# Pooling means by trailing sums on VectorE and the layer norm's scale taken behind the mix, in a two-layer float32 trunk on one core

## The reference, cut to what matters

```python
def spatial_gating(u, v, ln_g, ln_b, w_s, b_s):          # branch A
    v = layer_norm(v, ln_g, ln_b)                        # over 512 channels
    w = where(mask[None], w_s, 0)                        # 4 groups of 128x128, masked by chunks of 64
    mixed = einsum('gts,bnsgc->bntgc', w, vb) + b_s      # mixes 128 positions
    return u * mixed

def multiscale_pool(xb, w_pool, scale):                  # branch B, one window per group of 128 channels
    for g, win in enumerate((2, 4, 8, 16)):
        count = minimum(t + 1, win)
        pooled.append((csg - lagged) / count - xf[:, :, g])   # mean of the last win positions, minus x
    y = einsum('bsgc,gcd->bsgd', pooled, w_pool)
    return y * scale
```

## Time and profile before

| what | value |
|---|---|
| median of 3 runs | 1374.77 us (1374.53 to 1376.07) |
| the profiled execution | 1375.41 us, of which its span is 1373.6 us |
| TensorE's granted clock, mean | 0.997 |
| TensorE busy | 1363.1 us |
| VectorE busy | 690.6 us |
| ScalarE, GpSimd busy | 561.3 and 553.9 us |

### The profile page before, as it was taken

One profiled execution on the slowest core, in us unless ns is written; L12 is line 12 of the kernel. 1 busy time (PEld: TensorE's weight loads), 2 busy tenths in 40 slices (PEclk: granted clock), 3 DMA queues, 4 the chain that ended last, 5 costly groups with the idle time before them and its releaser, 6 DMA issues.

```text
span 1373.6 us, 16132 instructions
## 1 busy us (share of the span) xinstructions
PE 1363.1 (99%) x6508; PEld 1150.1 (84%) x6508; DVE 690.6 (50%) x1051; ACT 561.3 (41%) x871; POOL 553.9 (40%) x233
## 2 busy tenths in 40 slices
PE   8999999999999999999999999999999999999998
PEld 7888888888888888888888888888888888888887
DVE  6977455255543333255767574451555532243743
ACT  5554454355552222224443654542555422222241
POOL 1334242443434444445354342424433344444443
PEclk9999999999999999999999999999999999999999
DMA  7313122232223333333343222222222233333232
GB/s 208 97 54 108 55 85 81 89 92 78 92 77 92 94 106 92 108 104 94 93 126 97 70 92 63 90 64 92 92 78 77 88 96 92 100 101 107 95 102 95
DMA packets 75354, 127.60 MB, mean 93 GB/s; under 512 B 8848, under 2 KB 45968, under 8 KB 75280
## 3 DMA queue, kind: packets, MB, share of 16 engines
q1 hardware_dynamic: 74048, 126.02, 29.8%
q10 hardware_dynamic: 1232, 0.55, 0.1%
HBM read 124.45 MB, written 2.10 MB: 92 GB/s over the span
## 4 chain that ended last, share of the span: by engine, by line
PE 95%; DVE 3%; ACT 1%; DMA 1%; SPq 0%; issue 0%; POOL 0%; DVEq 0%; ACTq 0%
PE ps L484 30%; PE ps L486 30%; PE ps L485 30%; DVE n_t L1456 1%; PE ps L753 1%; PE ps L687 1%; PE ps L789 1%; PE ps L674 1%; ACT w_hi L961 0%; DMA x<-x_in 0%; DVE h_lo L1315 0%; SPq L399 0%; DMA par<-par_in 0%; PE ps L565 0%; DVE xh L1482 0%
## 5 line engine op out<-in xcount | busy, mean ns | idle before, releaser
L459 POOL TENSOR_TENSOR w_lo<-w_raw,w_hi 128x1024 fp32r<-128x1024 f32 x222 | 547.3, 2469 | 776.4 <-ACT w_hi L961 776.2
L484 PE MATMUL ps<-h_hi,w_hi 128*128 128x512 f32 (+1 forms) x1096 | 427.3, 390 | 0.7 <-POOL w_lo L459 0.7
L486 PE MATMUL ps<-h_hi,w_lo 128*128 128x512 f32 (+1 forms) x1096 | 425.2, 388 | 0.0
L485 PE MATMUL ps<-h_lo,w_hi 128*128 128x512 f32 (+1 forms) x1096 | 425.0, 388 | 0.0
L961 ACT ACTIVATE w_hi<-w_raw 128x1024 fp32r<-128x1024 f32 x227 | 238.3, 1054 | 169.5 <-PE ps L486 167.7
L484 PEld LDWEIGHTS ps<-h_hi,w_hi 128*128 128x128 f32 x1096 | 205.9, 188 | 42.5 <-issue 0.9
L486 PEld LDWEIGHTS ps<-h_hi,w_lo 128*128 128x128 f32 x1096 | 205.8, 188 | 42.5
L485 PEld LDWEIGHTS ps<-h_lo,w_hi 128*128 128x128 f32 x1096 | 205.9, 188 | 40.8
L1757 DVE SCALAR_TENSOR_TENSOR m_part<-th,ps 128x512 f32<-128x512 f32 x48 | 33.0, 687 | 236.9 <-PE ps L486 236.8
L1179 ACT ACTIVATE th<-ps 128x512 f32<-128x512 f32 x48 | 28.7, 597 | 182.0 <-PE ps L486 182.0
L484 PE MATMUL ps<-w_hi,act_hi 128*128 128x512 f32 (+1 forms) x192 | 74.8, 390 | 4.5 <-DVE w_lo L1315 4.5
(11 more groups left out here) (334 smaller groups left out, 1969.2 us busy)
## 6 DMA issues: line engine op xcount, KB each, us to landing
w_raw<-w_in SPq DMA_DIRECT2D x172, 512.0 KB, 3.5
w_raw<-w_in SPq DMA_DIRECT2D x124, 128.0 KB, 2.4
w_raw<-w_in SPq DMA_DIRECT2D x36, 256.0 KB, 3.1
x<-x_in SPq DMA_DIRECT2D x8, 256.0 KB, 5.9
w_raw<-w_in SPq DMA_DIRECT2D x32, 64.0 KB, 2.1
out_x<-x SPq DMA_DIRECT2D x7, 256.0 KB, 4.1
rows<-rows_in SPq DMA_DIRECT2D x2, 768.0 KB, 5.7
p_raw<-p_in SPq DMA_DIRECT2D x2, 512.0 KB, 4.4
```

What stands on the lines that cost most here:

```text
L459: pool.tensor_tensor(w_lo_t[s][:], w_raw_t[s][:], w_hi_t[s][:].bitcast(F32), ALU.subtract).then_inc(w_lo_made, 1)
L484: pe.matmul(o, a_hi, b_hi, start=first, stop=False, skip_group_check=skip)
L485: pe.matmul(o, a_hi, b_lo, start=False, stop=False, skip_group_check=skip)
L486: return pe.matmul(o, a_lo, b_hi, start=False, stop=last, skip_group_check=skip)
```

## The change

- The bx products read h (after `h_made`), with weights as the stationary operand, so that the result stands by features in bank g, in the order bx3, bx2, bx1, bx0. ScalarE copies each to `xb`, which has 16 zero columns ahead of each group.
- VectorE sums windows by doubling: `trail(g)` makes g + 1 adds of the array with itself shifted by 1, 2, 4 and 8 columns, corrects the first 16 columns by a table, and multiplies by 1/window and subtracts x. `windows`, `window_tables` and their tables go. The edge table is four small operations in `constants_taken`.
- `pool_high` and `pool_split` make the parts from `xb`, groups 3, 2, 1, 0; the pool products run as groups 0 to 3, after bz1.
- `norm_scaled` goes. The mixing products run on the plain normalized values; two products with a matrix of ones sum the mixing weights into bank 5, `mix_off` is that sum by the shift plus the bias, and `mix_t` is the product by the scale plus `mix_off`. Scale and shift come as columns by a transpose in `rope_rows`, copied to `ln_col`.
- The load of these rows moves from before av3 to before av2 on SP. Queues of ScalarE and VectorE are written in a new order.

```diff
-    names = [f"lat{i}" for i in range(4)] + [f"av{i}" for i in range(4)] + [f"bx{i}" for i in range(4)]
+    names = [f"lat{i}" for i in range(4)] + [f"av{i}" for i in range(4)] + [f"bx{i}" for i in (3, 2, 1, 0)]
...
-ROWS_BY = "av3"
+ROWS_BY = "av2"
...
-        bx_hi, bx_lo = plan(0, 16, ("bx_hi", [TB, SEQ], F32R), ("bx_lo", [TB, SEQ], F32R))
+        xb, trail_a, trail_b = plan(0, 13, ("xb", [G, WIN], F32), ("trail_a", [WIN], F32), ("trail_b", [WIN], F32))
...
-        vn_hi, vn_lo, rows = plan(36, 58, ("vn_hi", [TB, SEQ], F32R), ("vn_lo", [TB, SEQ], F32R),
-                                  ("rows", [3, SEQ], F32))
+        vn_hi, vn_lo, rows, mix_off, ln_t = plan(
+            36, 58, ("vn_hi", [TB, SEQ], F32R), ("vn_lo", [TB, SEQ], F32R), ("rows", [SEQ], F32),
+            ("mix_off", [G, P], F32), ("ln_t", [P], F32))
...
+            whole = {"bx": lambda: S_BX[i], "bz": lambda: S_BZ[i], "cz": lambda: S_CZ[i], "gb": lambda: S_M1 + 3 * i,
...
-                        sync.dma_start(rows[:], rows_in[l].partition_broadcast(P)).then_inc(rows_loaded, 16)
+                        sync.dma_start(ln_t[0:2 * G, :], rows_in[l, 0:2].rearrange("u (g p) -> (u g) p", p=P)).then_inc(
+                            rows_loaded, 16)
+                        sync.dma_start(rows[:], rows_in[l, 2].partition_broadcast(P)).then_inc(rows_loaded, 16)
...
+                pe.wait_ge(rows_loaded, (l + 1) * 32)
+                pe.transpose(ps[:, 2 * 512 + P:2 * 512 + P + 2 * G], ln_t[0:2 * G, :], ident[0:2 * G, 0:2 * G])
...
-            def windows(l, g, b):
...
-                pe.wait_ge(pool_made, after(l * G + g))
+                pe.wait_ge(pool_made, after(l * G + 3 - g))
...
-                for i in range(4):
-                    project_rows(l, f"bx{i}", i, hx_hi, hx_lo, 0)
+                for i in (3, 2, 1, 0):
+                    w_hi, w_lo = chunk(l, f"bx{i}")
+                    for k in range(KD):
+                        if i == 3:
+                            pe.wait_ge(h_made, after(l * KD + k))
+                        last = mm3(bank(i), w_hi[:, k, :], w_lo[:, k, :], tile(h_hi, k), tile(h_lo, k), k == 0,
+                                   k == KD - 1)
+                    last.then_inc(done(l, f"bx{i}"), 1)
...
-                pe.wait_ge(h_made, after(l * KD + KD - 1))
                 project(l, "bz0", 7)
                 w_hi, w_lo = chunk(l, "vp")
                 pe.wait_ge(lat_made, after(l * 3))
                 for t in range(TB):
-                    pe.wait_ge(bx_made, after(l * TB + t))
+                    pe.wait_ge(bx_copied, after(l * G + 3 - t))
                     mm3(bank(t), tile(ckvn_hi, t, P), tile(ckvn_lo, t, P), w_hi[:, 0:G, :],
                         w_lo[:, 0:G, :]).then_inc(v_ready, 1)
-                if l == 0:
-                    pe.wait_ge(windows_made, after(0))
+                project(l, "bz1", 4)
                 for g in range(G):
-                    if g < 3:
-                        pe.wait_ge(lat_made, after(l * 3 + g))
-                    else:
-                        pe.wait_ge(v_made, after(l * TB))
-                    windows(l, g, WINDOW_BANKS[g])
-                pe.wait_ge(v_made, after(l * TB + 1))
-                project(l, "bz1", 1)
+                    pe.wait_ge(v_made, after(l * TB + g))
+                    pool_product(l, g, g)
+                pe.wait_ge(lat_made, after(l * 3 + 2))
+                project(l, "bz2", 6)
+                w_hi, w_lo = chunk(l, "mix")
+                pe.matmul(bank(5), ones_r[:], w_hi[:, 0:G, :], start=True, stop=False)
+                pe.matmul(bank(5), ones_r[:], w_lo[:, 0:G, :], start=False, stop=True).then_inc(wsum_ready, 1)
+                pe.wait_ge(ln_made, after(l * TB + TB - 1))
                 for g in range(G):
-                    if g < 2:
-                        pe.wait_ge(v_made, after(l * TB + g + 2))
-                    pool_product(l, g, 2 + g)
-                project(l, "bz2", 6)
-                w_hi, w_lo = chunk(l, "mix")
-                pe.wait_ge(ln_made, after(l * TB + TB - 1))
-                for g, b in enumerate(MIX_BANKS):
-                    if g:
-                        pe.wait_ge(pooled, after(l * G + g - 1))
+                    pe.wait_ge(pooled, after(l * G + g))
                     for t in range(TB):
-                        last = mm3(ps[:, b * 512 + t * P:b * 512 + (t + 1) * P], vn_hi[:, t, g * P:(g + 1) * P],
+                        last = mm3(ps[:, g * 512 + t * P:g * 512 + (t + 1) * P], vn_hi[:, t, g * P:(g + 1) * P],
                                    vn_lo[:, t, g * P:(g + 1) * P], w_hi[:, g, :], w_lo[:, g, :])
                     last.then_inc(mix_ready if g < G - 1 else done(l, "mix"), 1)
-                pe.wait_ge(pooled, after(l * G + 3))
+                pe.wait_ge(off_made, after(l))
                 project(l, "bz3", 5)
...
-                        if t != 1:
-                            pe.wait_ge(mix_taken, after(l * G + max(t - 1, 0)))
+                        pe.wait_ge(mix_taken, after(l * G + t))
...
-                weights_up_to(l, "bx0")
+                weights_up_to(l, "bx3")
...
                         act.wait_ge(*end_of(l, "av2"))
-                        weights_up_to(l, "bx1")
+                        weights_up_to(l, "bx2")
                 act.wait_ge(*end_of(l, "av3"))
-                weights_up_to(l, "bx2")
+                weights_up_to(l, "bx1")
...
+                def copied(g):
+                    act.wait_ge(*end_of(l, f"bx{g}"))
+                    act.activation(xb[:, g, PAD:WIN], bank(g), ACT.Copy).then_inc(bx_copied, 1)
...
+                def pool_high(g):
+                    act.wait_ge(trail_made, after(l * G + 3 - g))
+                    act.activation(pool_hi[g][:], xb[:, g, PAD:WIN], ACT.Copy).then_inc(pool_hi_made, 1)
...
+                copied(3)
+                weights_up_to(l, "bx0")
                 act.wait_ge(ln_var, after(l))
                 act.activation(sm("ln_root"), sm("ln_root"), ACT.Sqrt).then_inc(ln_root, 1)
-                act.wait_ge(*end_of(l, "bx0"))
-                weights_up_to(l, "bx3")
-                def norm_high(t):
-                    act.wait_ge(ln_scaled, after(l * TB + t))
-                    act.activation(vn_hi[:, t, :], xh[:, t, :], ACT.Copy).then_inc(vn_hi_made, 1)
+                copied(2)
+                weights_up_to(l, "bz0")
                 norm_high(0)
                 norm_high(1)
-                act.wait_ge(*end_of(l, "bx1"))
-                weights_up_to(l, "bz0")
-                act.wait_ge(*end_of(l, "bx2"))
+                pool_high(3)
+                copied(1)
                 weights_up_to(l, "vp")
-                act.wait_ge(*end_of(l, "bx3"))
-                for t in range(TB):
-                    act.activation(bx_hi[:, t, :], bank(t), ACT.Copy, scale=sm("r", t)).then_inc(bx_hi_made, 1)
-                for u, (o, gain) in enumerate(((ckvn_hi[:], col(l, "ckv")), (cqn_hi[:, 0, :], col(l, "cq", 0)),
-                                               (cqn_hi[:, 1, :], col(l, "cq", 1)))):
-                    act.wait_ge(lat_ready, after(l * 3 + u))
-                    act.activation(o, bank(4 + u), ACT.Copy, scale=gain).then_inc(lat_hi_made, 1)
-                    if u == 0:
-                        weights_up_to(l, "bz1")
+                norm_high(2)
+                norm_high(3)
+                pool_high(2)
+                copied(0)
+                weights_up_to(l, "bz1")
+                latents_high(0, ckvn_hi[:], col(l, "ckv"))
+                latents_high(1, cqn_hi[:, 0, :], col(l, "cq", 0))
+                latents_high(2, cqn_hi[:, 1, :], col(l, "cq", 1))
+                pool_high(1)
...
-                for g in range(G):
-                    act.wait_ge(w_ready, after(l * G + (g if g < 2 else G - 1)))
-                    act.activation(pool_hi[g][:], bank(WINDOW_BANKS[g]), ACT.Copy).then_inc(pool_hi_made, 1)
-                norm_high(2)
-                norm_high(3)
-                bz(1, 1)
+                pool_high(0)
+                bz(1, 4)
                 weights_up_to(l, "mix")
...
+                for g in range(G):
+                    s = CC["inv_edge"].start + g * PAD
+                    dve.tensor_scalar(tile(edge, g, PAD), c_st[:, s:s + PAD], float(2 << g), None, ALU.mult)
...
-            def window_tables():
...
+                        dve.tensor_copy(sm("ln_col"), ps[:, 2 * 512 + P:2 * 512 + P + 2 * G])
...
-                if l == 0:
-                    window_tables()
-                def norm_scaled(t):
-                    settle(dve.tensor_tensor(xh[:, t, :], xh[:, t, :], rows[:, 0, :], ALU.mult))
-                    dve.tensor_tensor(xh[:, t, :], xh[:, t, :], rows[:, 1, :], ALU.add).then_inc(ln_scaled, 1)
+                def trail(g):
+                    w, cur = 2 << g, xb[:, g, :]
+                    dve.wait_ge(bx_copied, after(l * G + 3 - g))
+                    for s in range(g + 1):
```

(68 more changed lines are left out.)

78 lines of the change are left out of this document (22 added, 56 removed).

## The result

The changed kernel takes 1402.7 us (median of 4 runs, 1401.13 to 1403.05); the kernel before, on the same chip, 1375.42 us (4 runs). The ratio is 1.0197, 95% interval 1.0184 to 1.0209: 2% slower, where 0.3% faster was forecast. The profiled execution took 1403.05 us with a span of 1401.3 us.

What follows compares the result with a forecast made beforehand. The prediction took TensorE to bound the kernel: 9.86 + 0.90 - 1.1 - 2.86 - 2.6 = 4.2 us gained, taken off the median of 1374.77, gives 1370.6 us, 0.3% faster; range 1367.6 to 1375.4 us.

Steps and rivals of the forecast that it cites:

- Removed and added work: On TensorE in both layers: dropped windows save 9.86 us; sums of the mixing weights and a transpose add 1.1 us.
- the wait for bz0's weights: TensorE's 0.90 us wait in layer 0 for late weights of bz0, forecast to go.
- Wait 1: The bx products wait for the normalized input h: 2.29 us in layer 0, 0.57 in layer 1, together 2.86 us.
- Wait 2: The value products wait for VectorE's low part of the first latent: 1.6 and 1.0 us, together 2.6 us.
- the slower rival with dear shifted adds: VectorE's shifted adds cost more than unshifted; at twice 0.72 us each the kernel takes 1383.6 us; chance 0.08.
- the end of the normalization: Start of VectorE's chain to the latents: normalized tiles end at 71.64 us in layer 0, 747.09 in layer 1.
- Wait 3: Pool products: trail(0)'s last operation on VectorE starts just before a GpSimd subtraction, margin 0.05 us, so no wait.
- The clock: Rival: TensorE's clock falls after the two waits for the values, bringing back 4.1 us, to 1374.7 us; chance 0.06.
- Later edits at nothing: Dropping norm_scaled, adding mix_off and moving the rows load earlier cost TensorE nothing, at bz3 and first queries included.

Runs made afterwards that it cites:

- e1: Changed kernel with 2528 unused bytes ahead of the weight ring, putting ring and arena at their addresses before the change: 1375.37 us, ratio 1.0003.
- e2: Changed kernel with weight ring and arena moved by 128 bytes (ring at 122496): 1375.19 us, ratio 1.0003 to the kernel before.
- e4: Kernel before the change with weight ring and arena moved by 128 bytes (ring at 124928): 1400.9 us, ratio 1.0188.
- e6: Changed kernel with the weight ring 128 bytes behind a multiple of 256 and the arena at a multiple: 1380.88 us, ratio 1.0039.
- e7: Changed kernel with 128 bytes in front of x, so that all matrix operands lie at multiples of 256: 1375.02 us, ratio 1.000.
- e9: e1 with VectorE making the low half of the first latents ahead of group 1's trailing sum: 1374.07 us, ratio 0.9994 to the kernel before.
- e8: e1 with ScalarE's square root ahead of the high half of bx0's weights: 1370.37 us, ratio 0.9966 to the kernel before.

## Why the prediction was wrong, step by step

**Not in the prediction at all: the place.** "The bx products stay 96 of 512 columns with operands swapped: nothing", and the same was assumed silently of all other products. The removed and added tiles were looked at as work and not as bytes ahead of the ring. This step is the 27 us: products of 512 columns that take 0.2318 in place of 0.2272 us, 23.5 us in all, and the hole and the fallen clock at the start of layer 1. e1, e2 and e4 show it from both sides.

**Removed and added work: right.** 9.86 forecast, 9.62 measured; 1.1 against 1.25; the wait for bz0's weights went.

**Wait 1: right.** 2.86 forecast, 2.91 measured, with three holes in bx3 of layer 0.

**Wait 2: right in kind, mis-sized.** 2.6 forecast (1.6 and 1.0), 5.44 measured (2.73 and 2.71). The prices of the adds were right (0.69 to 0.70 each, shifted or not, so the slower rival with dear shifted adds is out), and so were three operations held up before the latent. The step that failed is the end of the normalization, "so they end at 71.64" and the 4.97 us carried over to layer 1: it priced the later table load and not the subtraction that the same move of the bx0 weights puts beside the variance operation, which then takes 2.1 us more in each layer. From the end of the last low half of h to the end of the normalization it is 8.56 and 8.55 us in e1; the forecast has 7.10 and 6.47. In layer 0 the table load is hidden behind the longer operation, so 1.5 us were missing there and 2.1 in layer 1; the rest of the chain gave back 0.3 to 0.4 in each. That the normalization of e1 ends at 71.81 and its values start at 90.01, where 71.64 and 90.0 were forecast, is luck: the front of e1 runs some 1.05 us ahead of the kernel before, from whose times the forecast counted.

**Wait 3: right.** In e1 the last operation of trail(0) started at 92.67, took 0.69 us, and GpSimd's subtraction at 92.72 came second, a margin of 0.05 us; in the changed kernel itself it is 94.52 and 94.57. A race won by so little is partly luck.

**The clock: a rival that was given too small a chance.** I gave 0.06 to a clock that falls after waits. After holes of 2.56 us it fell in layer 1 of e1 and not in layer 0; in e2 (two such holes) it was the other way round; in e6 it fell in both layers and in e7 in neither; after 2.3 us in the changed kernel it fell in layer 1 alone; after 1.98 us in e9 in both; after 0.80 and 0.87 us in e8 in none. Over all nine runs with a wait of 2.1 to 2.6 us at the values it fell after 9 of 18 such holes, and after 4 of the 6 holes of 1.6 us at the start of layer 1. The row of layer 0 in e1 from the values on, and then two of layer 1:

```profile
90.00:92.00 2.00, 1.99 (x9) 1.65 (x10) 2.00 (x4) 1.99 (x3) 0.00 (x0) 1.00 0.00 0
766.00:768.80 2.80, 2.71 (x9) 2.24 (x10) 2.73 (x6) 2.79 (x4) 0.01 (x1) 0.75 0.00 0
768.80:771.00 2.20, 2.20 (x7) 1.68 (x7) 2.17 (x4) 1.94 (x5) 2.20 (x1) 0.54 0.00 0
```

At the granted 0.50 that is 1.2 GHz, and each fall costs some 1.6 us, where the rival had 2.0. The Trainium skill, "TensorE: Matmul & The Clock Gate", section "What's actually happening", says that idleness halves the clock; these rows agree, and show that a hole of 1.6 us can be enough here, though not each time.

**Later edits at nothing: right.** Neither bz3 nor the first queries waited.

## What to carry to other kernels

Where a change adds or drops a tile, compare the addresses of all matrix operands before and after, not only the work; when products are longer at full clock in stages that nobody touched, pad the layout and time that alone before looking for another cause. When work moves to VectorE with both inputs in SBUF, lay every GpSimd instruction over it, the smallest operations too: a four-column one can cost 2 us. And a wait of 2 us on TensorE is best given a range up to nearly twice its length, since the clock can fall behind it.

## What the runs showed of the hardware that was not expected

- Products with 512 columns follow each other every 0.2272 us where all matrix operands lie at the same remainder of 256 bytes in SBUF (0 or 128, both tried), and the products concerned every 0.230 to 0.235 us where some lie 64 or 128 bytes off. Over a whole kernel bound by such products it was 2%. Products of 448 columns and fewer lost hardly anything. The Trainium skill, "SBUF — State Buffer", section "Who interferes with whom", says that TensorE never waits on anyone and that its two read ports are independent; the measurement differs, and decides. Its section "Operand start alignment" is by its own words about legality, not speed.
- A VectorE operation on 128x4 elements waits for a GpSimd subtraction as long as a 512-wide one does: 2.25 us in place of 0.16.
- The granted clock fell after some holes of 1.6 to 2.6 us and not after others of the same length; what decides between them was not found.
